# Gate and up weights of a two-expert MoE kernel in units of two k-tiles by 1024 columns, and the narrow expert's halves summed after transposes

## The chip, the cores and the metric

The kernel runs on one core of a Trainium2 chip. The metric is device time in microseconds (us), lower is better. The engines are named as in the profile: PE is TensorE (matmuls), PEld its weight loads, DVE VectorE, ACT ScalarE, POOL GpSimd, and SP the engine that issues the DMAs.

## The reference

A trunk of two layers on 256 tokens of width 1024, all in float32. Each layer has a token mixer (latent attention and stick-breaking attention) and a channel mixer. Layer 0's channel mixer is a dense SwiGLU. Layer 1's, in which the change lies, routes each token to two of eight experts of inner width 3584:

```python
def swiglu(x, w_gate, w_up, w_down):
    return (jax.nn.silu(x @ w_gate) * (x @ w_up)) @ w_down
...
    for e in range(N_EXPERTS):
        out = out + combine[:, e:e + 1] * swiglu(t, w_gate[e], w_up[e], w_down[e])
```

`w_gate[e]` and `w_up[e]` are 1024 by 3584, `w_down[e]` is 3584 by 1024, so one expert holds 44 MB and the eight hold 352 MB.

## The kernel before

**Precision.** A float32 product is made of single-pass products: a weight is split into a high part (ACT, `pair_hi_of`, L576) and a low part, raw minus high (DVE, `pair_lo_of`, L1262); the activations are split likewise. `product` (L1594 to L1596) issues high x high, high x low and low x high, three matmuls.

**Pairs.** Experts are handled in four pairs. The first of a pair is the wide one (`L`): up to 128 tokens, stationary operands `hg_hi` and `hg_lo`, 12 matmuls of 512 columns a unit. The second is the narrow one (`S`): up to 64 tokens, whose high and low halves stand side by side in one 128-wide stationary operand (`gs_pack`, later `f_pack`), so that a unit takes 8 matmuls; the two halves of its result stand in partitions 0 to 63 and 64 to 127 and must be added. Two overflow paths for fuller experts exist and are not run here.

**Units.** Weights come as units of 1 MB (128 partitions x 2048 floats), 42 to an expert and 84 to a pair. A gate or up unit is four k-tiles by 512 columns, so each partition gets four pieces of 2 KB; a down unit is two adjacent rows for each partition, one piece of 8 KB. SP issues one DMA a unit into a ring of seven raw buffers (`RAW`), each free again when its low part is made. The split parts go into four buffers (`PAIR_SPLIT`: three of `w_hi`/`w_lo` and `more_hi`/`more_lo`): the high part of unit j waits until PE has used unit j-4.

**Order.** `pair_order` lists the units for all engines. For each of seven chunks of 512 inner columns it has, wide expert first and then narrow: gate (2 units), up (2), and from chunk 1 on the down units of the chunk before (2). Both experts' last down units close the pair. So wide and narrow units alternate in runs of six. SP, ACT, DVE and PE each walk this list; the other work of ACT and DVE is hung behind the split of a certain unit (the `if u == ...` lines of their `pair`), and an engine does nothing else while it waits for such an item's input.

**Between the units.** For the wide expert: SiLU from PSUM (ACT L787), times up (DVE L1422), four transposes (PE L2000, `turn_l`), high part (ACT L791), low part (DVE L1426). For the narrow expert: both results are copied out of PSUM (ACT L796, L800), and `fold_s` (PE L2010) adds the halves and transposes in one step by eight float32 matmuls against a 0/1 matrix `fold`; then SiLU (ACT L804), times up (DVE L1432), high part (DVE L1437), low part (DVE L1439). Once in a pair come: the gather of the next wide tokens (`gather_l`, L1928, two halves), the gather of the narrow ones (`gather_s`, L1937), the scatter of the pair before (`scatter`, L1958 to L1961) with the weighting before it and four additions behind it (DVE L1412, L1414), and two selections (L1945, L1947) with the DVE's choice of the next pair's tokens (L1470, L1332).

**Start.** The first wide expert of all is the same whatever the routing says, so its units may be loaded early; before the first narrow unit SP must read the order of the experts (`order_i`, L480).

## Time and profile before

| | us |
|---|---|
| median of 3 runs | 1449.53 (1449.0 to 1451.09) |
| the profiled execution's own time | 1446.6 |
| its span (first to last instruction) | 1444.9 |
| PE busy / DVE busy / ACT busy | 1362.8 / 1261.7 / 940.7 |

The MoE of layer 1 runs from about 523 us to the end. "Busy" counts a matmul from its start to its modelled end, though the next one starts earlier; what a matmul costs in a stream is therefore the distance between two starts, not its duration. DVE and ACT instructions overlap a little too, by about 0.08 and 0.1 us.

### The profile page before, as it was taken

How to read it: one execution, taken by the hardware profiler on the slowest of the kernel's cores; microseconds unless marked ns; L12 is line 12 of the kernel's file. 1: busy time of each engine (PE TensorE's matmuls, PEld its weight loads, DVE VectorE, ACT ScalarE, POOL GpSimd, SP SyncE). 2: the span in 40 equal slices, each digit the busy share in tenths (PEclk: the TensorE clock that was granted, in tenths of full speed). 3: DMA queues.
4: the chain of work that ended last, by engine and by line, in shares of the span. 5: the costliest groups of instructions: out<-in, count | busy, mean ns of one | idle time of the engine just before them, and what ended most of it. 6: DMA issues, size and time to landing. Idle time of an engine off the chain costs nothing.

```text
span 1444.9 us, 18313 instructions
## 1 busy us (share of the span) xinstructions
PE 1362.8 (94%) x7090; PEld 1142.0 (79%) x7090; DVE 1261.7 (87%) x1141; ACT 940.7 (65%) x875; POOL 3.8 (0%) x35
## 2 busy tenths in 40 slices
PE   2899889999999889999999999999999999999995
PEld 2777789998887668887788887888888888888884
DVE  6878789887767779999998999998999998999997
ACT  1645443333437368878786888777878887877784
POOL 1000000000000000000000000000000000000000
PEclk9898999999899989999999999999999999999998
DMA  8973469987563139999999999999999999999992
GB/s 329 359 255 133 146 236 323 333 319 249 173 218 113 59 137 396 397 400 396 396 401 391 388 396 400 398 400 374 379 400 396 396 405 392 363 397 398 399 401 96
DMA packets 189596, 467.24 MB, mean 323 GB/s; under 512 B 8734, under 2 KB 10940, under 8 KB 175164
## 3 DMA queue, kind: packets, MB, share of 16 engines
q1 hardware_dynamic: 189500, 465.98, 86.3%
q8 instruction: 58, 0.95, 0.3%
q14 instruction: 38, 0.31, 0.1%
HBM read 464.90 MB, written 1.05 MB: 322 GB/s over the span
## 4 chain that ended last, share of the span: by engine, by line
PE 81%; DVE 8%; DMA 6%; ACT 3%; issue 1%; SPq 0%; DVEq 0%; ACTq 0%
PE bank L1594 17%; PE bank L1596 16%; PE bank L1595 16%; PE bank L1991 5%; PE bank L1992 5%; PE bank L2010 3%; PE bank L2034 3%; PE bank L2036 3%; DMA raw<-in_w_ex_down 3%; DVE w_lo L1262 3%; DMA raw<-in_w_ex_gate 2%; ACT w_hi L576 1%; DVE ring_sum L991 1%; PE bank L1928 1%; PE bank L1637 1%; PE bank L1615 1%
## 5 line engine op out<-in xcount | busy, mean ns | idle before, releaser
L1262 DVE TENSOR_TENSOR w_lo<-raw,w_hi 128x2048 fp32r<-128x2048 f32 x252 | 570.1, 2288 | 57.6 <-ACT w_hi L576 56.6
L576 ACT ACTIVATE w_hi<-raw 128x2048 fp32r<-128x2048 f32 x252 | 479.6, 1918 | 114.5 <-PE bank L1596 68.1
L1262 DVE TENSOR_TENSOR more_lo<-raw,more_hi 128x2048 fp32r<-128x2048 f32 x84 | 191.9, 2285 | 2.9 <-ACT more_hi L576 2.9
L552 ACT ACTIVATE w_hi<-raw 128x2048 fp32r<-128x2048 f32 (+1 forms) x54 | 102.3, 1897 | 130.5 <-PE bank L1596 121.4
L576 ACT ACTIVATE more_hi<-raw 128x2048 fp32r<-128x2048 f32 x84 | 161.3, 1920 | 33.6 <-PE bank L1596 20.3
L920 DVE TENSOR_TENSOR w_lo<-raw,w_hi 128x2048 fp32r<-128x2048 f32 (+1 forms) x54 | 121.7, 2258 | 19.6 <-ACT w_hi L552 19.4
L1594 PE MATMUL bank<-w_hi,hg_hi 128*128 128x512 f32 x336 | 136.5, 406 | 2.2 <-DVE w_lo L1262 1.6
L1991 PE MATMUL bank<-w_hi,gs_pack 128*128 128x512 f32 x336 | 135.2, 402 | 0.0
L1596 PE MATMUL bank<-w_hi,hg_lo 128*128 128x512 f32 x336 | 132.9, 396 | 0.0
L1595 PE MATMUL bank<-w_lo,hg_hi 128*128 128x512 f32 x336 | 132.9, 395 | 0.0
L1992 PE MATMUL bank<-w_lo,gs_pack 128*128 128x512 f32 x336 | 132.7, 395 | 0.0
L1594 PE MATMUL bank<-h_hi,w_hi 128*128 128x256 f32 x448 | 128.3, 286 | 1.6 <-DVE gate_m L969 1.6
L1595 PE MATMUL bank<-h_lo,w_hi 128*128 128x256 f32 x448 | 126.8, 283 | 0.0
L1596 PE MATMUL bank<-h_hi,w_lo 128*128 128x256 f32 x448 | 126.7, 283 | 0.0
L1594 PEld LDWEIGHTS bank<-h_hi,w_hi 128*128 128x128 f32 x448 | 86.0, 192 | 4.2 <-DVE gate_m L969 3.2
L1594 PE MATMUL bank<-w_hi,e_hi 128*128 128x512 f32 x224 | 88.9, 397 | 0.0
L1595 PE MATMUL bank<-w_lo,e_hi 128*128 128x512 f32 x224 | 88.6, 396 | 0.0
L1596 PE MATMUL bank<-w_hi,e_lo 128*128 128x512 f32 x224 | 88.6, 395 | 0.0
L1595 PEld LDWEIGHTS bank<-h_lo,w_hi 128*128 128x128 f32 x448 | 86.1, 192 | 0.7 <-issue 0.5
L1596 PEld LDWEIGHTS bank<-h_hi,w_lo 128*128 128x128 f32 x448 | 85.9, 192 | 0.0
L1594 PEld LDWEIGHTS bank<-w_hi,hg_hi 128*128 128x128 f32 x336 | 63.2, 188 | 21.6 <-issue 6.3
L991 DVE SCALAR_TENSOR_TENSOR ring_sum<-raw,cols,ring_sum 128x512 f32<-128x512 f32 x98 | 73.6, 751 | 3.3
(316 smaller groups left out, 2470.5 us busy)
## 6 DMA issues: line engine op xcount, KB each, us to landing
raw<-in_w_ex_gate SPq DMA_DIRECT2D x112, 1024.0 KB, 11.9
raw<-in_w_ex_up SPq DMA_DIRECT2D x112, 1024.0 KB, 12.3
raw<-in_w_ex_down SPq DMA_DIRECT2D x112, 1024.0 KB, 12.7
raw<-in_w_ada SPq DMA_DIRECT2D x48, 1024.0 KB, 7.0
raw<-in_w_in SPq DMA_DIRECT2D x12, 1024.0 KB, 6.5
raw<-in_w_ff_gate SPq DMA_DIRECT2D x10, 1024.0 KB, 7.0
raw<-in_w_ff_up SPq DMA_DIRECT2D x10, 1024.0 KB, 6.9
raw<-in_w_ff_down SPq DMA_DIRECT2D x10, 1024.0 KB, 6.3
```

Of the source, the lines that this page charges most:

```text
L552: act_e.activation(w_hi[:, s % SPLIT, 0:words], raw[:, n % RAW, 0:words], ACT.Copy).then_inc(hi_done, 1)
L576: act_e.activation(dst, raw[:, (N0 + n) % RAW, :], ACT.Copy).then_inc(hi_done, 1)
L920: dve.tensor_tensor(w_lo[:, s % SPLIT, 0:words], raw[:, n % RAW, 0:words], w_hi[:, s % SPLIT, 0:words].bitcast(F32), ALU.subtract).then_in ...
L991: ins = dve.scalar_tensor_tensor(out=dst, in0=w[:, k, :], scalar=ck, in1=dst, op0=ALU.mult, op1=ALU.add)
L1262: dve.tensor_tensor(lo, raw[:, (N0 + n) % RAW, :], hi.bitcast(F32), ALU.subtract).then_inc(lo_done, 1)
L1594: mm(o, lh, rh, start=first, stop=False, skip_group_check=True)
L1595: mm(o, lh, rl, start=False, stop=False, skip_group_check=True)
L1596: return mm(o, ll, rh, start=False, stop=last, skip_group_check=True)
L1991: mm(bank[b][:, :], gs_pack[:, kk, :], wh[:, k, :], start=kk == 0, stop=False, skip_group_check=True)
L1992: last = mm(bank[b][:, :], gs_pack[:, kk, :], wl[:, k, :], start=False, stop=kk == 7, skip_group_check=True)
L2010: last = mm(bank[2][:, o:o + HALF], pre[:, a * P:(a + 1) * P], fold[:, :], start=(i, a) == (0, 0), stop=True, skip_group_check=True)
L2034: mm(bank[6 + half][:, :], f_pack[:, kk, :], wh[:, k, cs], start=c == 0 and kk == 0, stop=False, skip_group_check=True)
```

## The change

Gate and up units become two k-tiles by 1024 columns: each partition gets two pieces of 4 KB. The inner width is cut into blocks of 1024, 1024, 1024 and 512 columns (`blocks`); the last keeps four k-tiles by 512. A block of 1024 has four gate, four up and four down units, so wide and narrow units now alternate in runs of eight (block 0), twelve (blocks 1 and 2) and eight (block 3), with two and two down units at the end. An accumulator is two PSUM banks wide; a pair of banks is gate accumulator, target of the transposes and narrow accumulator by turns. SiLU, the product, the evacuations and the splits of a block are one instruction 1024 wide. `turn_l` makes eight transposes a block and stands ahead of the narrow gate units instead of behind them.

`fold_s` still runs once for each 512 columns, now as eight transposes of 128 x 128; the halves then stand in adjacent columns, ACT copies the lower ones out (`keep_low_part`) and DVE adds (`sum_s`). The high part of the narrow activation moves from DVE to ACT (`high_s`). Folds 0 and 1 follow wide units of block 1, folds 2 to 5 the first and the fourth narrow down unit of blocks 1 and 2, fold 6 the first narrow down unit of block 3; copy and sum come four units behind a fold, SiLU and product six, the split eight. In block 1 and 2 the second fold waits for the first one's sum. Evacuations, gathers and selections are hung on other units; `add_rows` goes behind the second narrow up unit of block 0. The SBUF for this comes from a smaller scratch area for DMAs issued by POOL, of which there are none.

```diff
+    blocks = [(0, 4), (1024, 4), (2048, 4), (3072, 2)]
+    NB, LAST_B = len(blocks), len(blocks) - 1
     pair_order = []
-    for c in range(EC):
+    for b, (_, n) in enumerate(blocks):
         for who in "LS":
-            pair_order += [(who, kind, c, half) for kind in ("gate", "up") for half in range(2)]
-            if c > 0:
-                pair_order += [(who, "down", c - 1, half) for half in range(2)]
-    pair_order += [(who, "down", EC - 1, half) for who in "LS" for half in range(2)]
+            pair_order += [(who, kind, b, i) for kind in ("gate", "up") for i in range(n)]
+            if b > 0:
+                pair_order += [(who, "down", b - 1, i) for i in range(blocks[b - 1][1])]
+    pair_order += [(who, "down", LAST_B, i) for who in "LS" for i in range(blocks[LAST_B][1])]
     PU = len(pair_order)
     pair_at = {u: j for j, u in enumerate(pair_order)}
+    last_of = lambda who, kind, b: pair_at[who, kind, b, blocks[b][1] - 1]
+    fold_after = {0: pair_at["L", "gate", 1, 1], 1: pair_at["L", "up", 1, 0], LAST: pair_at["S", "down", LAST_B - 1, 0]}
+    for b in range(1, LAST_B):
+        fold_after[2 * b], fold_after[2 * b + 1] = pair_at["S", "down", b - 1, 0], pair_at["S", "down", b - 1, 3]
+    fold_at = {j: c for c, j in fold_after.items()}
+    sum_at = {j + 4: c for c, j in fold_after.items()}
+    silu_at = {j + (6 if c < LAST else 5): c for c, j in fold_after.items()}
+    split_f_at = {j + (8 if c < LAST else 6): c for c, j in fold_after.items()}
+    fold_banks = (6, 2, 0, 2)
+    gather_bank = lambda n, half: 3 if half == 0 else (2 if n == 0 else 1)
...
-        bank = [ctx.enter_context(nc.psum_tensor(f"bank{i}", [P, 512], F32)) for i in range(8)]
+        two_banks = [ctx.enter_context(nc.psum_tensor(f"banks{2 * i}", [P, 1024], F32)) for i in range(4)]
+        bank = [two_banks[i // 2][:, (i % 2) * 512:(i % 2 + 1) * 512] for i in range(8)]
...
+        def gate_banks(b):
+
+
+            return of_block(two_banks[b % 2], b)
+
+        def up_banks(b):
+
+            return of_block(two_banks[1 - b % 2], b)
+
+        def narrow_up_banks(b):
+
+            return gate_banks(b) if b < LAST_B else bank[3]
...
+                else:
+                    w = w_ex_gate if kind == "gate" else w_ex_up
+                    k = KD // units
+                    src = w[0, bass.ds(e, 1), i * k * P:(i + 1) * k * P, c0:c0 + UNIT // k].rearrange(
+                        "o (k p) n -> p (o k) n", p=P)
+                    dst = raw[:, slot, :].rearrange("p (k n) -> p k n", k=k)
...
+                def keep_low_part(c):
+
+                    act_e.wait_ge(folded, p * EC + (c + 1))
+                    if p > 0 or c > 1:
+                        act_e.wait_ge(flo_done, p * EC + c - 1)
+                    parts = two_banks[fold_banks[c // 2] // 2][:, :].rearrange("p (k t) -> p k t", t=P)
+                    act_e.activation(f_sum[:, c % 2, :, :], parts[:, :, HALF:P], ACT.Copy).then_inc(flow_kept, 1)
 
                 def silu_s(c):
-                    act_e.wait_ge(folded, p * EC + (c + 1))
-                    act_e.activation(f_act[:, :, :], bank[2][:, 0:4 * HALF].rearrange("p (k t) -> p k t", t=HALF),
-                                     ACT.Silu).then_inc(fsilu, 1)
+                    act_e.wait_ge(fsum_done, p * EC + (c + 1))
+                    act_e.activation(f_sum[:, c % 2, 0:4, :], f_sum[:, c % 2, 0:4, :], ACT.Silu).then_inc(fsilu, 1)
+
+                def high_s(c):
+                    act_e.wait_ge(fact_done, p * EC + (c + 1))
+                    act_e.activation(f_pack[:, 4 * (c % 2):4 * (c % 2) + 4, 0:HALF], f_sum[:, c % 2, 0:4, :],
+                                     ACT.Copy).then_inc(fhi_done, 1)
...
                         pair_hi_of(p, j)
+                    if j in sum_at:
+                        keep_low_part(sum_at[j])
+                    if j in silu_at:
+                        silu_s(silu_at[j])
+                    if j in split_f_at:
+                        high_s(split_f_at[j])
...
+                def sum_s(c):
+
+                    dve.wait_ge(flow_kept, p * EC + (c + 1))
+                    parts = two_banks[fold_banks[c // 2] // 2][:, :].rearrange("p (k t) -> p k t", t=P)
+                    dve.tensor_tensor(f_sum[:, c % 2, :, :], parts[:, :, 0:HALF], f_sum[:, c % 2, :, :],
+                                      ALU.add).then_inc(fsum_done, 1)
 
                 def gated_s(c):
 
                     dve.wait_ge(fsilu, p * EC + (c + 1))
-                    dve.tensor_tensor(f_act[:, :, :], f_act[:, :, :],
-                                      bank[2][:, 4 * HALF:8 * HALF].rearrange("p (k t) -> p k t", t=HALF),
+                    dve.tensor_tensor(f_sum[:, c % 2, 0:4, :], f_sum[:, c % 2, 0:4, :], f_sum[:, c % 2, 4:8, :],
                                       ALU.mult).then_inc(fact_done, 1)
-                    dve.wait_ge(fact_done, p * EC + (c + 1))
-                    h, l = f_pack[:, :, 0:HALF], f_pack[:, :, HALF:P]
-                    dve.tensor_copy(h, f_act[:, :, :]).then_inc(fhi_done, 1)
+
+                def low_s(c):
+                    k = slice(4 * (c % 2), 4 * (c % 2) + 4)
                     dve.wait_ge(fhi_done, p * EC + (c + 1))
-                    dve.tensor_tensor(l, f_act[:, :, :], h.bitcast(F32), ALU.subtract).then_inc(flo_done, 1)
+                    dve.tensor_tensor(f_pack[:, k, HALF:P], f_sum[:, c % 2, 0:4, :], f_pack[:, k, 0:HALF].bitcast(F32),
+                                      ALU.subtract).then_inc(flo_done, 1)
 
...
                 def fold_s(c):
 
-                    pe.wait_ge(gate_kept, p * EC + (c + 1))
-                    pe.wait_ge(up_kept, p * EC + (c + 1))
+                    b, o = c // 2, 512 * (c % 2)
+                    pe.wait_ge(gate_kept, p * NB + (b + 1))
+                    pe.wait_ge(up_kept, p * NB + (b + 1))
+                    if c == 0 and p > 0:
+                        pe.wait_ge(acc_done, p * 4)
+                    if c % 2 == 1:
+                        pe.wait_ge(fsum_done, p * EC + c)
+                    if b == LAST_B:
+                        pe.wait_ge(elo_done, p * NB + (b + 1))
                     for i, pre in enumerate((g_pre, u_pre)):
                         for a in range(4):
-                            o = (4 * i + a) * HALF
-                            last = mm(bank[2][:, o:o + HALF], pre[:, a * P:(a + 1) * P], fold[:, :], start=(i, a) == (0, 0),
-                                      stop=True, skip_group_check=True)
+                            last = pe.transpose(bank[fold_banks[b] + i][:, a * P:(a + 1) * P],
+                                                pre[:, o + a * P:o + (a + 1) * P], ident[:, :])
                     last.then_inc(folded, 1)
 
-                def down_l(c):
-                    for pair_of in range(2):
-                        pe.wait_ge(elo_done, p * EC + (c + 1))
-                        wh, wl = unit(("L", "down", c, pair_of))
...
+                def done(u, last):
+                    last.then_inc(split_used, 1)
+                    if pair_at[u] in fold_at:
+                        fold_s(fold_at[pair_at[u]])
...
+                for b, (_, units) in enumerate(blocks):
+
+                    if p > 0 or b > 0:
+                        pe.wait_ge(gate_kept, p * NB + b)
+                    for i in range(units):
+                        into_l("gate", b, i, gate_banks(b))
+
+                    if b == 1:
+                        pe.wait_ge(up_kept, p * NB + 1)
+                    elif p > 0 or b > 0:
+                        pe.wait_ge(fsum_done, p * EC + 2 * b)
+                    for i in range(units):
+                        into_l("up", b, i, up_banks(b))
+                        if (b, i) == (0, 1):
+                            pe.wait_ge(esilu, p * NB + (b + 1))
+                            gather_s(p)
+                        if (b, i) == (SEL_L, 2):
...
                     else:
-                        if c == 1 and p > 0:
+                        if b == 1 and p > 0:
                             pe.wait_ge(acc_done, p * 4)
-                        down_l(c - 1)
-                        pe.wait_ge(flo_done, p * EC + c)
-                    into_s("gate", c, 2)
-                    turn_l(c)
-                    if c == SEL_L:
-                        selection(sel, now, tl_ready)
-                    if c == SEL_S:
-                        selection(sel_s, now_s, ts_ready)
-                    if c == LAST and p + 1 < PAIRS:
...
-                fold_s(LAST)
-                if p + 1 < PAIRS:
-                    gather_l(p + 1, 1)
-                down_l(LAST)
-                down_s(LAST)
+                        if b == LAST_B and p + 1 < PAIRS:
+                            gather_l(p + 1, 0)
+                            gather_l(p + 1, 1)
+                        for i in range(blocks[b - 1][1]):
+                            down_l(b - 1, i)
+                    if b == SEL_L:
+                        pe.wait_ge(tl_done, p * 2 + 2)
+                    if b == SEL_S:
+                        pe.wait_ge(ts_done, p * 2 + 2)
+                    turn_l(b)
+                    for i in range(units):
+                        into_s("gate", b, i, up_banks(b))
+                    if b < LAST_B:
+                        pe.wait_ge(elo_done, p * NB + (b + 1))
+                    elif p + 1 < PAIRS:
+                        pe.wait_ge(hgl_done, (p + 1) * 2 + 1)
+                    for i in range(units):
+                        into_s("up", b, i, narrow_up_banks(b))
+                    if b > 0:
+                        for i in range(blocks[b - 1][1]):
+                            down_s(b - 1, i)
+                for i in range(blocks[LAST_B][1]):
+                    down_l(LAST_B, i)
```

PE, around the second fold of a block. Before, in chunk 2 of the first pair (`hg_hi` marks wide units, the fold is L2010):

```order
L2010 MATMUL bank<-fold,g_pre 128x64 x4
L2010 MATMUL bank<-fold,u_pre 128x64 x4
L1594 MATMUL bank<-w_hi,hg_hi 128x512
L1595 MATMUL bank<-w_lo,hg_hi 128x512
L1596 MATMUL bank<-w_hi,hg_lo 128x512
```

After, at the end of block 1's narrow run (`f_pack` marks narrow down units):

```order
L2121 MATMUL banks<-more_hi,f_pack 128x512
L2123 MATMUL banks<-more_lo,f_pack 128x512
L2060 MATMUL banks<-ident,g_pre 128x128 x4
L2060 MATMUL banks<-ident,u_pre 128x128 x4
L1669 MATMUL banks<-w_hi,hg_hi 128x512
```

A fold is still eight rows of PE's order; it stood among wide units and now stands between narrow down units or behind the last of them.

DVE, in the narrow run of chunk 1 and the wide one of chunk 2 before (the splits are L1262, `more_lo` is every fourth of them):

```order
L1439 TENSOR_TENSOR f_pack<-f_act,f_pack 128x4x64
L1262 TENSOR_TENSOR w_lo<-raw,w_hi 128x2048 x2
L1422 TENSOR_TENSOR e_act<-e_act,bank 128x512
L1262 TENSOR_TENSOR more_lo<-raw,more_hi 128x2048
L1262 TENSOR_TENSOR w_lo<-raw,w_hi 128x2048
L1470 COPY now<-place 128x4
L1332 TENSOR_SCALAR sel<-slot_no,now 128x128 x2
L1262 TENSOR_TENSOR w_lo<-raw,w_hi 128x2048 x2
L1426 TENSOR_TENSOR e_lo<-bank,e_hi 128x512
```

After, from the fourth narrow unit of block 1 to the sum behind its first narrow fold (`f_sum<-banks`):

```order
L1326 TENSOR_TENSOR more_lo<-raw,more_hi 128x2048
L1492 TENSOR_TENSOR e_lo<-banks,e_hi 128x1024
L1326 TENSOR_TENSOR w_lo<-raw,w_hi 128x2048
L1544 COPY now<-place 128x4
L1396 TENSOR_SCALAR sel<-slot_no,now 128x128 x2
L1326 TENSOR_TENSOR w_lo<-raw,w_hi 128x2048 x2
L1326 TENSOR_TENSOR more_lo<-raw,more_hi 128x2048
L1326 TENSOR_TENSOR w_lo<-raw,w_hi 128x2048 x3
L1326 TENSOR_TENSOR more_lo<-raw,more_hi 128x2048
L1326 TENSOR_TENSOR w_lo<-raw,w_hi 128x2048
L1499 TENSOR_TENSOR f_sum<-banks,f_sum 128x512
```

From the fourth narrow unit to the sum there are ten splits, one `e_lo`, one choice of tokens and the sum.

## Rows read from the trace of the kernel before

**Rows 1.** Pairs 1, 2: length, busy PE PEld DVE ACT POOL, clock, DMA share, GB/s.

```profile
757.93:982.93 225.00, 224.63 (x1075) 184.09 (x1074) 210.73 (x137) 177.91 (x131) 0.00 (x0) 1.00 1.04 395
982.93:1208.10 225.17, 224.65 (x1075) 184.09 (x1074) 211.09 (x137) 178.15 (x131) 0.00 (x0) 1.00 1.03 391
```

**Rows 2.** Chain of waits that ended last: start us, us, what.

```profile
522.96 6.50 PE bank L1928 x32
...
757.93 3.52 PE bank L1937 x32
...
907.52 1.73 PE bank L2010 x16
...
924.25 0.44 PE bank L2000 x4
...
938.03 1.73 PE bank L2010 x16
...
955.19 1.79 PE bank L1928 x16
...
966.16 1.84 PE bank L1928 x16
...
1002.01 2.39 DVE acc L1414 x4
...
1425.93 0.70 ACT ye_hi L756
```

**Rows 3.** PE in order of time: start us, us, instruction, from 700 us.

```profile
700.29 0.40 PE L1991 MATMUL bank<-w_hi,gs_pack 128*128 128x512 f32 x1
...
701.92 0.39 PE L1992 MATMUL bank<-w_lo,gs_pack 128*128 128x512 f32 x1
...
704.77 0.47 PE L2034 MATMUL bank<-more_hi,f_pack 128*128 128x512 f32 x1 [0.59 <-DVE more_lo L1262]
```

**Rows 4.** PE in order of time, the selection of pair 2.

```profile
1026.72 0.38 PE L1945 MATMUL bank<-ident,sel 128*128 128x128 f32 x2
...
1027.31 0.48 PE L1991 MATMUL bank<-w_hi,gs_pack 128*128 128x512 f32 x1
```

**Rows 5.** DVE in order of time.

```profile
702.34 2.28 DVE L1262 TENSOR_TENSOR more_lo<-raw,more_hi 128x2048 fp32r<-128x2048 f32 x1
...
1029.18 0.68 DVE L1426 TENSOR_TENSOR e_lo<-bank,e_hi 128x512 fp32r<-128x512 f32 x1
1029.78 2.28 DVE L1262 TENSOR_TENSOR more_lo<-raw,more_hi 128x2048 fp32r<-128x2048 f32 x1
...
1038.59 2.29 DVE L1262 TENSOR_TENSOR more_lo<-raw,more_hi 128x2048 fp32r<-128x2048 f32 x1
...
1055.07 0.16 DVE L1470 COPY now<-place 128x4 f32<-128x4 f32 x1
...
1055.66 4.49 DVE L1262 TENSOR_TENSOR w_lo<-raw,w_hi 128x2048 fp32r<-128x2048 f32 x2
```

**Rows 6.** ACT in order of time.

```profile
1045.30 1.92 ACT L576 ACTIVATE w_hi<-raw 128x2048 fp32r<-128x2048 f32 x1 [0.73 <-PE bank L1596]
1048.10 1.92 ACT L576 ACTIVATE more_hi<-raw 128x2048 fp32r<-128x2048 f32 x1 [0.88 <-PE bank L1596]
```

**Rows 7.** Groups of one pair period by form, DVE and ACT: busy us, mean ns.

```profile
L1439 DVE TENSOR_TENSOR f_pack<-f_act,f_pack 128x256 fp32r<-128x256 f32 x7 | 3.0, 426 | 0.2
...
L791 ACT ACTIVATE e_hi<-bank 128x512 fp32r<-128x512 f32 x7 | 4.1, 591 | 0.0
...
L804 ACT ACTIVATE f_act<-bank 128x256 f32<-128x256 f32 x7 | 2.7, 383 | 5.5 <-PE bank L2010 5.5
```

**Rows 8.** DMA, 600 to 700 us: GB/s in slices of 2.5 us.

```profile
GB/s 419 390 385 389 384 414 420 390 389 385 387 401 421 408 390 384 390 383 420 423 383 389 384 389 407 423 406 380 388 386 392 421 402 393 385 388 385 425 423 381
```

**Rows 9.** SP: its first DMAs of a narrow unit, and its wait before them.

```profile
527.42 0.96 SPq L459 DMA_DIRECT2D raw<-in_w_ex_gate  x2
...
SPq L480 <- DVE order_i L1365: 35.8, 1, 35.8
```

More of the change, by code:

```diff
@@ L1457, in pair @@
[L1457 to L1467 removed]
+                    if u[0:2] == ("L", "down") and i == 2:
+                        gated_l(b + 1)
@@ new lines, in turn_l, with down_l @@
+                def turn_l(b):
+                    pe.wait_ge(ea_done, p * NB + (b + 1))
+                    for a in range(2 * blocks[b][1]):
+                        last = pe.transpose(gate_banks(b)[:, a * P:(a + 1) * P], e_act[:, a * P:(a + 1) * P], ident[:, :])
+                    last.then_inc(e_tp, 1)
+                def down_l(b, i):
+                    pe.wait_ge(elo_done, p * NB + (b + 1))
+                    wh, wl = unit(("L", "down", b, i), 2)
+                    for half in range(2):
+                        for k in range(2):
+                            kk = 2 * i + k
+                            cs = slice(half * 512, (half + 1) * 512)
+                            last = product(bank[4 + half][:, :], e_hi[:, kk, :], e_lo[:, kk, :], wh[:, k, cs], wl[:, k, cs],
+                                           b == 0 and kk == 0, b == LAST_B and kk == 3)
+                    done(("L", "down", b, i), last)
```

334 lines of the change are left out of this document (161 added, 173 removed).

## The prediction

> **What bounds the kernel now.** I read the stretches of the pairs first. A middle pair lasts 225.0 or 225.2 us, and in it PE is busy for 224.6, DVE for 210.7 and ACT for 177.9, while the DMA engines are at full share with 391 to 395 GB/s [rows 1]. The chain of waits runs almost wholly along PE [rows 2]. So PE sets the pace, DMA and DVE stand close behind, and ACT has room.
>
> Next, what PE does with a pair, by the distance between starts. In a stream a matmul of 512 columns starts each 0.233 us (seven steps in 1.63 us, [rows 3]), so a wide unit costs 12 x 0.233 = 2.80 and a narrow one 8 x 0.233 = 1.87. A pair has 42 of each: 195.7 us. Seven folds of 1.73 are 12.1, seven times four transposes of 0.44 are 3.1, the two halves of gather_l 1.79 + 1.84 = 3.6, gather_s 3.5 [rows 2], the scatter's 16 matmuls 3.7, two selections of 0.59 each 1.2 [rows 4]. The sum is 222.9, so PE waits for about 2.2 us a pair. A chunk shows where: from fold to fold it takes 938.03 - 907.52 = 30.5 us [rows 2], its work 6 x 2.80 + 6 x 1.87 + 1.73 + 0.44 = 30.2, which leaves 0.3, six times a pair.
>
> These waits can be derived, and I use the derivation for the new order too. The split of a unit needs a buffer that PE has left four units earlier. Let t = 0 be the moment at which a narrow run begins. ACT learns of a used buffer 0.3 later (a matmul's duration of 0.40 against 0.233, and a hand-over of 0.15, which is what lies between the end of a low part, 702.34 + 2.28, and the matmul at 704.77) [rows 3, 5]. The fourth narrow unit's high part therefore runs from 0.3 to 2.2 (1.92 each, [rows 6]) and its low part starts at 2.25. From there DVE needs 2.20 for each split (8.81 for four) and 0.60 for e_lo [rows 5]. In the old run of six, DVE still has four splits and one e_lo to do before the next wide unit can start: 2.25 + 8.8 + 0.6, and 0.23 for its last end and the hand-over, is 11.9; PE's own work is 0.44 + 6 x 1.87 = 11.65. Wait 0.25: the trace has 0.3.
>
> **The change, part by part.**
>
> The folds. Eight transposes take the place of eight float32 matmuls. Four transposes cost 0.44 [rows 2], so eight are 0.88 against 1.73: 0.85 x 7 = 5.95 us a pair, 24 in all. The bounds are 0.88 (nearest row, taken) and 1.73 (as before, nothing won). turn_l keeps its 28 transposes a pair. PE's own work falls to 216.9.
>
> The DMAs. The bandwidth goes up and down with the units: about 387 GB/s for two thirds of the time, about 420 for one third [rows 8], which is how 2 KB gate/up pieces and 8 KB down pieces share a pair. A unit thus takes 1.049 MB / 387 = 2.71 or 2.50 us, and a pair 56 x 2.71 + 28 x 2.50 = 221.8. A 4 KB piece is not in these rows; its bounds are the two rates. At the better one the floor falls to 8 x 2.71 + 76 x 2.50 = 211.7, at the worse it stays. Both are below the pair length found below, and DMA has seven raw buffers to even things out, so I put this part at 0. What it should do is end most of ACT's waits for DMA.
>
> The Trainium skill ("DMA: Bandwidth & Descriptors", section "Where 436 GB/s comes from") says that a load from HBM is limited to about 358 GB/s a core; by that a pair's 88.1 MB would need 246 us and nothing on PE could help. The trace disagrees, with 391 to 395 GB/s over whole pairs [rows 1], and the measurement decides.
>
> DVE and ACT. DVE loses the high part of f (0.3 x 7) and gains a sum of the size of e_lo (0.60 x 7); for e_act and e_lo I need 1024 columns: 256 take 0.43 and 512 take 0.68 [rows 5, 7], so 1024 take about 1.20 by the slope (two separate ones, 1.36, is the other bound), 1.12 from start to start. DVE stays near 212 us a pair. ACT gains a copy of 0.59 and one of 0.38 for each fold and loses some overhead, about 5 us a pair on 178 [rows 1, 7]. Averages thus say nothing: 217 on PE, 212 on DVE, 212 on DMA, 183 on ACT.
>
> The longer runs. Here the gain goes. In a run of twelve wide units DVE is ahead but can bank only four buffers; in a run of twelve narrow ones PE needs a unit each 1.87 and DVE makes one each 2.20. Blocks 1 and 2: turn_l now stands first (0.88), then eight narrow units, the ninth, a fold, three more, the second fold. Ahead of the second fold PE's own work is 0.88 + 12 x 1.87 + 0.88 = 24.2. That fold waits for the first one's sum, and DVE's order has, from 2.25 on, ten splits (22.0), e_lo (1.12), the choice of tokens (0.59, [rows 5]) and the sum (0.60), then 0.23: 26.8. PE loses 2.6 in each of the two blocks, most of it spread over single units, the last 0.9 at the fold. The next wide unit is ready by then.
>
> Block 0: the scatter (3.7) hides the product gated_l. After it PE has 0.88 + 8 x 1.87 = 15.8. The fifth narrow unit's high part waits for the first to be used (0.88 + 1.87 + 0.3 = 3.05), its low part ends at 7.2; then come a split, add_rows (2.39, [rows 2]), and three splits up to the next wide unit: 7.2 + 2.2 + 2.4 + 6.6 + 0.23 = 18.6. Loss 2.8. Block 3 with the closing down units: PE 0.44 + 8 x 1.87 + 0.88 + 5.6 + 3.7 = 25.6; DVE 2.25 + ten splits 22.0 + e_lo 0.6 + sum 0.6 + product and low part 0.7 + 0.23 = 26.4. Loss 0.8. Together 2.8 + 2.6 + 2.6 + 0.8 = 8.8 against 2.2 before. I keep 0.4 for what my derivation does not explain now (2.2 less six times 0.3): 216.9 + 8.8 + 0.4 = 226.1, 1.0 more than before.
>
> The other pairs. Pair 0 goes from 529.5 (the end of gather_l) to 757.9 - 5.6 = 752.3, 222.9 us. After: no scatter, so 213.2, but turn_l now has nothing to hide behind: gated_l follows the low part of the third narrow unit, whose high part may start 2.8 before the wide run ends; it is done 3.4 after that end, so PE loses 3.5; then 0.3 instead of 2.8 (no add_rows), 5.2, 0.8, 0.4: 223.4, 0.5 more. In this pair SP stops for 35.8 us for the order of the experts and goes on at 527.4 [rows 9]; four units are in by then, after the change seven or eight, so DMA can't hold it up. The last pair goes from 1208.1 - 5.6 to 1425.9, 223.4 us. After: no gather_l, 213.3; waits 2.8, twice 2.0 (no choice of tokens), 0.4 at the end, where the f work no longer stands behind the last split, and 0.4: 220.9, 2.5 less.
>
> **The sum.** 0.5 + 1.0 + 1.0 - 2.5 = 0: 24 us won on the folds, 24 lost in waits. The profiled execution took 1446.6 (span 1444.9 and 1.7 around it), and the median is 1449.5, 2.9 higher; I forecast 1450 for the median.
>
> **Rivals.**
>
> A: PE keeps its pace. If the narrow runs cost no more waiting than now (2.2 a pair), all 24 us are won: 1426. For it: PE is 99.8% busy and DVE's queue shows idle 14 us a pair [rows 1]. Against it: these 14 us lie in the wide runs, where DVE waits for buffers. Half of it gives 1438.
>
> B, slower: DMA paces the narrow runs. Twelve units at 2.50 to 2.71 are 30 to 32.5 us against my 27.7 (26.8 and the fold). If the seven raw buffers are nearly empty when a narrow run begins, each of the blocks 1 and 2 loses about 4 more: 8 x 4 = 32, 1482. It decides at about two landed units. For it: DMA is at full share now. Against: PE's waits and gathers leave it 4 to 14 us a pair after the change.
>
> C, slower: a fold's transposes of g_pre and u_pre cost as much as its matmuls did; then the waits partly cover it (the fold's end matters twice a block): about +15, 1465.
>
> D: PE's clock. The granted clock is 1.00 in both pairs [rows 1] though each has 32 transposes and small waits. If it fell to 1.2 GHz in the narrow runs for a third of their length, each run of twelve would lose 7 us: over 1490. The Trainium skill ("TensorE: Matmul & The Clock Gate", section "Part 4: PE-mode transpose") says that transposes don't count as PE activity the way matmuls do; the change adds 56 of them a pair and waits next to them. By that rule D would come; the transposes of the present kernel bear nothing of it out.
>
> **Chances.** Forecast 0.58 (own range 1444 to 1457), A 0.24, B 0.10, C 0.05, D 0.03. About 0.2% (2.9 us) is what a measurement can tell from no change. The forecast's share splits into faster 0.10, same 0.27, slower 0.21, since each wait may be wrong by 0.5 us and there are 13 of them. Faster is then 0.34, same 0.27, slower 0.39. The range 1434 to 1464 takes in the upper half of A and the lower edge of C and leaves out about 0.2.
>
> **What would show it.** Right: folds of about 0.88; PE waiting for low parts in the second half of narrow runs and for the sum before each second narrow fold, 7 to 10 us a pair; ACT's waits for DMA nearly gone and a DMA share below 1; narrow runs of blocks 1 and 2 near 27.7 us. Wrong: PE's waits at 2 to 4 us a pair (A), ACT waiting for DMA in narrow runs (B), folds of 1.7 (C), a granted clock below 1 there (D).

## The result, and the profile after

The changed kernel takes 1457.89 us (median of 4 runs, 1457.07 to 1458.39); the kernel before, on the same chip, 1449.26 (4 runs). The ratio is 1.0065, 95% interval 1.005 to 1.008: slower by 8.6 us, where I had forecast no change. The profiled executions are 1457.07 and 1446.6.

First the stretches of pairs 1 and 2, from one gather of the narrow rows to the next, as in [rows 1] (columns: length, busy PE, PEld, DVE, ACT, POOL with their instructions, granted clock, DMA share, GB/s):

```profile
771.91:999.30 227.39, 221.65 (x1017) 176.26 (x1016) 212.08 (x131) 182.63 (x132) 0.00 (x0) 1.00 0.98 382
999.30:1226.70 227.40, 221.66 (x1017) 176.25 (x1016) 211.97 (x131) 182.64 (x132) 0.00 (x0) 1.00 0.99 388
```

A middle pair has grown by 2.3 us, though its seven folds have 56 matmuls fewer. PE is no longer busy all the time, and the DMA share has gone from 1.04 to 0.98. The chain of waits that ended last, over the whole kernel and by engine, was 81% PE, 8% DVE and 6% DMA before. Now:

```profile
PE 65%; DVE 29%; ACT 4%; issue 1%; DMA 1%; SPq 0%; DVEq 0%; ACTq 0%
```

In its order of time it shows a fold of eight transposes with 0.87, where [rows 2] has 1.73. In the narrow run of block 1 in pair 2 it follows DVE for 26 us, up to the second fold, which waits for the first one's sum:

```profile
581.83 0.87 PE banks L2060 x8
...
1067.09 1.93 ACT more_hi L621
1069.04 2.29 DVE more_lo L1326
1071.34 1.14 DVE e_lo L1492
1072.47 2.20 DVE w_lo L1326
1074.78 0.48 DVE sel L1396 x2
1075.27 4.40 DVE w_lo L1326 x2
1079.67 2.20 DVE more_lo L1326
1081.87 6.60 DVE w_lo L1326 x3
1088.48 2.20 DVE more_lo L1326
1090.68 2.20 DVE w_lo L1326
1092.88 0.61 DVE f_sum L1499
1093.63 1.07 PE banks L2060 x8
```

This is the prediction's derivation almost item by item: the fourth unit's high part, ten splits of 2.20, e_lo with 1.14 (1.12 taken), the choice of tokens, the sum with 0.61 (0.60 taken). ACT's waits for DMA among all waits of 560 to 1410 us are four lines with 3.1 us in all; before it was 43.4 us.

```profile
ACT more_hi L621 <- DMA raw<-in_w_ex_up: 1.3, 2, 0.6
...
ACT w_hi L621 <- DMA raw<-in_w_ex_up: 0.7, 1, 0.7
...
ACT more_hi L621 <- DMA raw<-in_w_ex_gate: 0.6, 1, 0.6
...
ACT w_hi L621 <- DMA raw<-in_w_ex_gate: 0.5, 1, 0.5
```

**Where the difference lies.** The beginning of the pair stage is a poor anchor: PE's first wide unit starts between 528.6 and 534.4 us in the fourteen profiled executions, though the code ahead of it is the same. So all executions below are measured by the *pair stage*, from the start of the first wide unit to the first matmul of the last scatter. It is 900.4 us before (529.22 to 1429.59) and 909.8 after (528.57 to 1438.38): 9.4 more. The rest of the 10.5 us between the two profiled executions lies outside it: 0.7 less ahead of the stage and 1.7 more behind its end. Pair by pair, first wide unit to first wide unit (for the last pair to the end of its units):

| | before | predicted | after |
|---|---|---|---|
| pair 0 | 222.9 | 223.4 | 226.5 |
| pairs 1 and 2, each | 225.1 | 226.1 | 227.4 |
| last pair | 223.4 | 220.9 | 223.2 |
| then PE's wait before the scatter | 3.7 | 3.7 | 5.2 |

The misses are 3.1 + 1.3 + 1.3 + 2.3 + 1.5 = 9.5 us. Most of them come from three things that the prediction lacks, each with its rows here.

First, a wait in block 3, in every pair. PE in order of time at the end of block 2 and in block 3 of pair 2, and DVE beside it:

```profile
1155.60 0.63 PE L2060 MATMUL banks<-ident,g_pre 128*128 128x128 f32 x4 [0.70 <-DVE f_sum L1499]
...
1163.05 0.50 PE L1669 MATMUL banks<-w_hi,hg_hi 128*128 128x512 f32 x1 [0.79 <-DVE f_sum L1499]
```

```profile
1160.11 2.28 DVE L1326 TENSOR_TENSOR more_lo<-raw,more_hi 128x2048 fp32r<-128x2048 f32 x1
1162.32 0.68 DVE L1499 TENSOR_TENSOR f_sum<-banks,f_sum 128x512 f32<-128x512 f32 x1
```

Block 3 has two gate units instead of four. Its first wide up unit therefore reaches the banks of fold 5 when DVE has only now come to that fold's sum, which stands four units behind it. Start to start, the matmul comes 0.95 us late.

Second, TensorE's clock. In pair 0 the turn of the wide product waits 3.4 us, as predicted (3.5). But the matmuls after it are 0.43 us apart instead of 0.233, which goes with the lower of the clock's two levels (1.2 instead of 2.4 GHz). The chain shows the distance, and the stretches of 3 us show the granted clock (the column behind POOL):

```profile
559.79 0.43 PE banks L2091
560.21 0.43 PE banks L2092
```

```profile
552.00:555.00 3.00, 2.77 (x12) 1.88 (x10) 0.99 (x1) 2.53 (x3) 0.00 (x0) 1.00 1.00 400
555.00:558.00 3.00, 0.00 (x0) 0.00 (x0) 3.00 (x4) 1.78 (x1) 0.00 (x0) 1.00 0.34 87
558.00:561.00 3.00, 2.82 (x12) 2.56 (x13) 2.36 (x3) 1.02 (x1) 0.00 (x0) 0.59 0.82 311
561.00:564.00 3.00, 3.00 (x13) 2.40 (x12) 1.11 (x1) 1.21 (x1) 0.00 (x0) 0.84 0.89 281
564.00:567.00 3.00, 3.00 (x15) 2.41 (x14) 2.25 (x2) 3.00 (x3) 0.00 (x0) 1.00 0.17 68
```

The eight transposes behind the wait take 1.60 here, where `a_last` and `a_five` below, with the clock at 1.00, have 1.06 and 1.07. From the first of these transposes to the end of 25 matmuls it is 8.3 us, in those two 6.7: the fall costs 1.6 us. Behind block 0's wait of 2.0 us in the last pair the same thing costs 1.5 us (eight matmuls at 0.43), with the clock at 0.65 and 0.79 from 1254 to 1260; pairs 1 and 2 have two small waits at this place instead, 0.5 us together.

Third, the tail. DVE's last split ends 2.2 us before PE's last unit does, and behind it stand the two sums over acc and x, ahead of the low parts that the scatter needs:

```profile
1428.65 2.29 DVE L1326 TENSOR_TENSOR more_lo<-raw,more_hi 128x2048 fp32r<-128x2048 f32 x1
1430.86 2.29 DVE L1563 TENSOR_TENSOR acc<-acc,gate_f 128x2048 f32<-128x2048 f32 x1
1433.18 2.29 DVE L1565 TENSOR_TENSOR x<-x,acc 128x2048 f32<-128x2048 f32 x1
1435.51 1.41 DVE L1448 SCALAR_TENSOR_TENSOR ye_lo<-banks,w_slot,ye_hi 128x512 fp32r<-128x512 f32 x2
```

Before, DVE came to these two sums 4 us before PE's last unit ended, and they cost nothing.

### The profile page after: what moved, and what is told of

It is laid out like the page before. It is cut to its first block, busy times and chain, and to the rows that moved or that the text cites. A ratio compares the mean times of both kernels' runs of the same rounds, so it can differ in the third digit from the quotient of the medians.

```text
span 1455.3 us, 17840 instructions
## 1 busy us (share of the span) xinstructions
PE 1351.9 (93%) x6866; PEld 1113.4 (77%) x6866; DVE 1265.6 (87%) x1117; ACT 958.2 (66%) x883; POOL 3.2 (0%) x32
## 4 chain that ended last, share of the span: by engine, by line
PE 65%; DVE 29%; ACT 4%; issue 1%; DMA 1%; SPq 0%; DVEq 0%; ACTq 0%
PE banks L1669 17%; PE banks L1671 17%; PE banks L1670 17%; DVE w_lo L1326 16%; DVE more_lo L1326 7%; ACT more_hi L621 2%; DVE ring_sum L1055 1%; PE banks L2003 1%; PE banks L1712 1%; PE banks L1690 1%; PE banks L2012 1%; PE banks L1869 1%; DVE e_lo L1492 1%; DMA raw<-in_w_ada 1%; PE banks L2060 1%
## 5 line engine op out<-in xcount | busy, mean ns | idle before, releaser
L2091 PE MATMUL banks<-w_hi,gs_pack 128*128 128x512 f32 x336 | 137.0, 408 | 8.1 <-DVE w_lo L1326 7.5
L1669 PE MATMUL banks<-w_hi,hg_hi 128*128 128x512 f32 x336 | 135.5, 403 | 3.8 <-DVE f_sum L1499 3.2
L2092 PE MATMUL banks<-w_lo,gs_pack 128*128 128x512 f32 x336 | 133.9, 398 | 0.0
L1671 PE MATMUL banks<-w_hi,hg_lo 128*128 128x512 f32 x336 | 132.8, 395 | 0.0
L1670 PE MATMUL banks<-w_lo,hg_hi 128*128 128x512 f32 x336 | 132.8, 395 | 0.0
L1669 PE MATMUL banks<-h_hi,w_hi 128*128 128x256 f32 x448 | 128.2, 286 | 1.6 <-DVE gate_m L1033 1.6
L1670 PE MATMUL banks<-h_lo,w_hi 128*128 128x256 f32 x448 | 126.7, 283 | 0.0
L1671 PE MATMUL banks<-h_hi,w_lo 128*128 128x256 f32 x448 | 126.7, 283 | 0.0
L1669 PEld LDWEIGHTS banks<-h_hi,w_hi 128*128 128x128 f32 x448 | 86.0, 192 | 4.3 <-DVE gate_m L1033 3.2
L1670 PEld LDWEIGHTS banks<-h_lo,w_hi 128*128 128x128 f32 x448 | 86.0, 192 | 0.7 <-issue 0.5
```

What stands on the lines that cost most here:

```text
L1669: mm(o, lh, rh, start=first, stop=False, skip_group_check=True)
L1670: mm(o, lh, rl, start=False, stop=False, skip_group_check=True)
L1671: return mm(o, ll, rh, start=False, stop=last, skip_group_check=True)
L2091: mm(at[:, cs], gs_pack[:, kk, :], wh[:, k, cs], start=kk == 0, stop=False, skip_group_check=True)
L2092: last = mm(at[:, cs], gs_pack[:, kk, :], wl[:, k, cs], start=False, stop=kk == 7, skip_group_check=True)
```

## The experiments

Each ratio is to the kernel before on the same chip; the stage is the pair stage of the profiled execution (before 900.4, after 909.8).

**1 to 3: the parts of the change in the old order.** `b_half_fold` takes half of each fold away from the kernel before (0.87 us, about what the transposes save; the product takes the gate part twice); `b_4kb` gives it the new pieces; `b_both` has both.

```
-   for i, pre in enumerate((g_pre, u_pre)):          b_half_fold
+   for i, pre in enumerate((g_pre,)):
+   if c < EC - 1:                                    b_4kb
+       r0 = (2 * (c % 2) + half) * 256
+       src = w[0, bass.ds(e, 1), r0:r0 + 256, c // 2 * 1024:(c // 2 + 1) * 1024]   # two k-tiles
```

> The kernel before, with one edit: fold_s does only its four matmuls on g_pre, and the product takes the gate part twice, so u_pre is not folded. PE's work falls by 0.87 a fold, as it does with eight transposes, and nothing is added on ACT or DVE; the order of the units and the 2 KB pieces stay. Theory (PE sets the pace and the DMA floor of 221.8 us a pair lies 3 us below it): pairs of 222 us instead of 225, 12 us less in all (9 to 15), ACT waiting for DMA more than now. Rival (the DMA floor doesn't bind): pairs of 219, 24 us less.

> The kernel before, with one edit: the gate and up units of chunks 0 to 5 are loaded as two k-tiles by 1024 columns, 4 KB pieces, the same bytes of HBM in all as the changed kernel reads, but used as if they were four k-tiles by 512, so the values are wrong and the work on them is the same. Theory (PE sets the pace before, DMA is hidden but for part of pair 0): 0 to 4 us less, ACT's waits for DMA nearly gone. Rival (DMA paces the kernel before): pairs of 212 to 216 us, 36 us or more less.

> Both edits together on the kernel before: half a fold, and 4 KB pieces used as if they were 2 KB ones (wrong values, same work). Theory (two limits close together, each hides the other): pairs of 219 us, 24 us less in all (20 to 28), clearly more than the two edits alone add up to. Rival (something else, DVE or ACT, already stands at 222): no more than half the fold alone gives, 9 to 15 us less.

Measured: 1446.8 (ratio 0.9978, 0.996 to 0.9996), 1445.42 (0.998, 0.9963 to 0.9997) and 1425.64 (0.9827, 0.9791 to 0.9863); stages 899.0, 898.2, 879.0. So each part alone is worth 1 to 3 us (medians, ratios and stages differ by that much), and both together 22.6. In `b_half_fold` my theory failed by its size, 12 us expected: as soon as PE needs less, DMA paces the kernel. Its middle pair, and ACT's three longest waits for DMA (us in total, times, longest):

```profile
756.78:979.98 223.20, 219.44 (x1019) 177.38 (x1018) 211.22 (x137) 178.33 (x131) 0.00 (x0) 1.00 1.04 396
```

```profile
ACT w_hi L576 <- DMA raw<-in_w_ex_up: 34.0, 44, 0.8
ACT w_hi L576 <- DMA raw<-in_w_ex_gate: 22.8, 43, 0.8
ACT w_hi L576 <- DMA raw<-in_w_ex_down: 20.8, 34, 1.2
```

This is close to the floor of 221.8 us a pair that the prediction worked out for 2 KB pieces: the gathers of the narrow rows of the four pairs lie 222.1, 223.2 and 224.6 us apart. In `b_4kb` ACT has no wait for DMA left, and the page's slices of 36 us, in which 4 KB and 8 KB pieces stand mixed, read 412 to 414 GB/s at the start of the pair stage (the sixteenth to nineteenth of forty). [rows 8] alternates between about 387 and 420:

```profile
GB/s 331 359 257 131 146 246 312 334 314 255 171 216 117 59 140 412 414 413 413 401 409 326 403 414 412 400 386 344 395 413 411 405 384 371 366 411 411 406 404 40
```
With both:

```profile
751.53:971.06 219.53, 218.67 (x1019) 177.69 (x1018) 210.13 (x137) 178.28 (x131) 0.00 (x0) 1.00 1.02 404
971.06:1190.68 219.62, 218.64 (x1018) 177.68 (x1018) 210.19 (x137) 178.09 (x131) 0.00 (x0) 1.00 1.01 401
```

The middle pairs are 5.5 us shorter than before, against the 5.95 that the folds were said to save. DMA is close again: ACT's waits for it are 39.9 us in all. The change has both savings too, and its stage is 30.8 us longer than this one's. What differs is the order of the work, runs of six there and of up to twelve here, with other items between the splits. No run has the long runs without the other items, so how the 30.8 us share out between the two is not shown.

**4: what a fold costs now.** The transposes of each fold made twice:

```
-   for i, pre in enumerate((g_pre, u_pre)):
+   for i, pre in 2 * list(enumerate((g_pre, u_pre))):
```

> The changed kernel, with every fold's eight transposes made twice: 0.87 us more PE work a fold, 6.1 a pair, 24 in all. Theory (in the narrow runs of blocks 1 and 2 DVE paces, so PE work ahead of a wait costs nothing): folds 2 and 4 are covered by the wait of the fold that follows, fold 5 by the wait of the wide up unit behind it, fold 6 half; the rest shows: 3 us a pair, 12 in all (9 to 15) over the changed kernel, 1470. Rival (PE paces everywhere): 24 us over it, 1482.

Measured: 1469.0 (1.0136, 1.0097 to 1.0176), 11 us above the changed kernel; stage 920.4. A fold of sixteen reads 1.75 in the chain. Rival C is out: the folds are at 0.87, and what they save is real, since giving it back costs 11 us, near the 12 expected, even with waits beside it.

**5, 6: the reserve of split buffers.** `PAIR_SPLIT` 3 and 5 for 4, in the changed kernel.

> The changed kernel with three pairs of split buffers (hi and lo) instead of four in the pair stage, nothing else. Theory (in a narrow run VectorE makes a split every 2.25 us and TensorE uses a unit up every 1.75, so every run of ten or more narrow units ends in waits, shortened by what the buffers hold in reserve at its start): one buffer less is one split less in reserve, 2.2 us more of waiting in each of the three full narrow runs of a pair and 1 to 2 in the short fourth: 8 us a pair, 33 on the kernel, 1491. Rival (reserve is not what it is about; TensorE waits for what stands between the splits, folds and row additions): under 8 us more, at most 1466.

> The changed kernel with five pairs of split buffers instead of four, the space taken from x and from one of the seven raw buffers (six are left); it leaves the residual x out of the last sum. Theory: one more split in reserve takes up to 2.2 us of waiting from each of the three full narrow runs, which now wait 2.6 to 2.9 us; 6 to 7 us a pair, so that the middle pairs take 220.5 to 221.5 us instead of 227.4, 25 us on the kernel, 1433. Against it stands the raw buffer that is missing: a transfer has one unit (1.8 us) less of lead. Rival (the waits follow VectorE's order of work, not its reserve): the middle pairs keep 225 us or more.

Measured: 1549.96 with three (1.0703, 1.0685 to 1.0721), 1446.04 with five (0.9992, 0.9977 to 1.0006); stages 1000.6 and 897.0. The direction is the theory's in both, but both sizes are wrong. With three the kernel loses 92 us, not 33, and the rival's 8 are out. (The paces in its expectation, 2.25 and 1.75, are not the trace's: it has 2.20 and 1.87.) DVE's waits for a high part grow from 47 us to 129 (first line), and ACT's share of the chain from 4% to 8%:

```profile
DVE w_lo L1326 <- ACT w_hi L621: 129.4, 118, 6.7
```

```profile
PE 65%; DVE 24%; ACT 8%; issue 2%; DMA 1%; SPq 0%; DVEq 0%; ACTq 0%
```

An estimate from the prediction's numbers says why: with three buffers a high part is ready 1.87 + 0.3 + 1.92 = 4.1 us after the low part three units before it, and DVE wants it after 2 x 2.20 = 4.4. So nearly every copy or SiLU of ACT in between delays it, and my derivation has DVE alone in the line. No run takes ACT's items out of it. With five the stretches of pairs 0 to 2 are:

```profile
548.53:768.23 219.70, 215.74 (x1002) 173.99 (x1001) 205.68 (x125) 181.59 (x132) 0.00 (x0) 1.00 1.00 395
768.23:992.24 224.01, 220.06 (x1018) 176.77 (x1017) 211.38 (x131) 180.13 (x132) 0.00 (x0) 1.00 0.99 389
992.24:1218.05 225.81, 220.23 (x1018) 176.76 (x1018) 212.46 (x131) 184.17 (x133) 0.00 (x0) 1.00 1.00 393
```

The first is 6.8 us shorter than in the changed kernel, but half of that is luck: 1.9 are a shorter wait at the turn (1.47 idle instead of 3.41) and 1.6 the fall of the clock, which doesn't come. The long narrow runs give 1.3 each and not 2.2: block 1 of pair 2 has one wait of 0.24 ahead of its second fold where there were 1.3, and the fold's own 0.9 stays. Pairs 1 and 2 are 3.4 and 1.6 us shorter; the second, 225.8, is what the rival said. There ACT's waits for DMA are back, with 43.5 us in all, and PE waits in wide units for what comes late by them, up to 1.4 us at a time. With six raw buffers and a high part wanted one unit earlier, the run can't say which of the two brings these waits, nor what five would give with seven raw buffers; there is no room for both.

**7, 8: single items.** `a_sum` makes the sum of fold 5 earlier; `a_add` moves the row additions from the narrow run to the wide one.

```
-   sum_at = {j + 4: c for c, j in fold_after.items()}                       a_sum
+   sum_at = {j + (2 if c == LAST - 1 else 4): c for c, j in fold_after.items()}
-   if u == ("S", "up", 0, 1) and p > 0:  add_rows(p - 1)                     a_add
+   if u == ("L", "gate", 1, 0) and p > 0:  add_rows(p - 1)
```

> The changed kernel with ScalarE's copy and VectorE's sum of fold 5 put two units behind the fold instead of four. Theory: in the last, short block the wide up unit that takes over the fold's banks waits 0.95 us for that sum in each pair, since VectorE comes to it only after a split that it makes too late; with the sum ahead, that wait goes in all four pairs: 3.8 us less, 1454. Rival (VectorE is behind there anyway, so that the wait turns up at the next unit): within 1 us of 1458.

> The changed kernel with VectorE's addition of a pair's rows to the sum (2.6 us of VectorE) moved from the first narrow run of the next pair to the wide run behind it. Theory: block 0's wait (2.9 us in the middle pairs, and 2.0 us in the last, behind which TensorE's granted clock fell and cost 1.6 more) goes but for 0.3 of it, for VectorE has time to spare in a wide run: 2.5 us in each of pairs 1 and 2, 3.5 in the last, 8.5 less, 1449. Rival (the wait is the narrow run's own shortfall and only shows behind the addition): pair 1 and 2 keep 226.5 us or more, 3 us less in all at most.

Measured: `a_sum` 1455.53 (1.0066, 1.0044 to 1.0087), stage 905.6, 4.2 less than after. In its trace the wait of 0.95 is gone from each pair and nothing comes in its place, so the first missed item is shown by the stage, with its size. The time of the whole kernel doesn't show it: the ratio is that of the changed kernel (1.0065). `a_add` 1456.44 (1.0067, 1.005 to 1.0084), stage 906.8, 3.0 less, and again no gain in the ratio. Its theory failed, and its rival was nearer. Block 0's wait of 2.0 is gone, but the next wide run has a new one:

```profile
1034.12 0.50 PE L1669 MATMUL banks<-w_hi,hg_hi 128*128 128x512 f32 x1 [1.47 <-DVE w_lo L1326]
```

At the end of a narrow run DVE has nothing in hand, and it gets only 0.6 us ahead for each wide unit (2.80 less 2.20). An item right behind the run costs nearly what it cost in it, here 1.6 instead of 2.0. In the last pair the clock stayed at 1.00 behind this shorter wait, and there 1.5 us were won.

**9 to 12: putting them together.** `a_p0` moves the first pair's product. `a_most` has `a_sum`, `a_p0`, the choice of tokens late in the next wide run, and the tail's two sums in wide runs of the last pair. `a_best` adds the row additions, four units into the wide run, and folds 0 and 1 two units later. `a_last` corrects the first pair:

```
-   if u == ("S", "up", SEL_L, 0) and p + 1 < PAIRS:           a_most
+   if u == ("L", "up", SEL_L + 1, 3) and p + 1 < PAIRS:
-   if u == ("S", "up", SEL_S, 0) and p + 1 < PAIRS:
+   if u == ("L", "down", SEL_S, 1) and p + 1 < PAIRS:
-   if u == ("S", "up", 0, 1) and p > 0:                       a_best (add_rows)
+   if u == ("L", "gate", 1, 3) and p > 0:
-   fold_after = {0: pair_at["L", "gate", 1, 1], 1: pair_at["L", "up", 1, 0],
+   fold_after = {0: pair_at["L", "gate", 1, 3], 1: pair_at["L", "up", 1, 2],
-   if u == ("S", "gate", 0, 2):                               a_last (evacuate_s, split_s, gated_l)
+   if u == ("S", "gate", 0, 1 if p == 0 else 2):
```

> The changed kernel in which, in the first pair alone, VectorE makes block 0's wide product behind the split of the second narrow gate unit; it stood behind the third and behind the split of the gathered narrow rows. Theory (the first pair is 3 us longer than the sum had it because TensorE waits 3.6 us at the turn of the wide product and its granted clock then falls to 0.59 for a few us, which costs 2 more): the product is ready about 3.4 us sooner, the wait is under 0.5 us, the clock stays at 1.00, and the first pair (from its first gather of narrow rows to the next) takes 221.5 to 222.5 us instead of 226.5: 4.5 us less, 1453.5. Rival 1 (the fall of the clock has nothing to do with the wait): 3 us less, and matmuls 0.43 us apart are there still. Rival 2 (VectorE's work is only shifted, and the wait turns up at the end of the narrow run): under 1.5 us less.

> The changed kernel with four moves on VectorE: the sum of fold 5 two units behind the fold; the first pair's product as in a_p0; the choice of tokens for the next pair taken out of the narrow runs and put late into the next wide run (blocks 2 and 3), where VectorE waits 0.5 us before each split; and in the last pair the two sums over acc and x, 2.3 us each, out of the tail into the wide runs of blocks 2 and 3. Theory, by its terms: 1.0 us in each of four pairs, 4.5 in the first pair, 0.6 to 0.7 in each of two narrow runs of three pairs, 1.5 in the tail: 4 + 4.5 + 3.9 + 1.5 = 13.9 less, 1444; middle pairs 225.1 instead of 227.4. Rival (work moved on VectorE comes back as a wait a run later, as it did where the row additions were moved): half of it, 1451, middle pairs 226.3 or more.

> As a_most, and VectorE's addition of the rows moved into the wide run of block 1, not at its start, where it cost 1.6 us of the 2.0 that it saved, but behind the split of its fourth unit, with folds 0 and 1 two units later so that they need not wait for it. Theory (what decides is whether VectorE has got ahead again before the work comes: four wide units give back 0.5 us each): of block 0's 2.9 us of waiting 2.0 go in each of pairs 1 to 3, at most 0.7 comes back in the wide run, and in the last pair the fall of the clock behind that wait goes too (1.6 us): 5.5 less than a_most, 1438.5. Rival (nothing is got ahead, the wait only moves): within 2 us of a_most.

> As a_best, with another order in the first pair's block 0: ScalarE's copy and VectorE's low part of the gathered narrow rows, and then the wide product, all one unit earlier (behind the second narrow gate unit). In a_p0 and a_best the product alone was moved, and TensorE's wait at the turn grew from 3.6 to 4.4 us, for TensorE waits there for the low part of the narrow rows too, which then stood behind the product and another split. Theory: with neither of them behind the third split, whose buffer TensorE frees only after the gather, the wait falls from 4.4 to about 1.4 us, which is the product alone; with a wait that short TensorE's granted clock stays at 1.00 there (0.9 us of matmuls 0.43 us apart go as well): the first pair 221.5 instead of 225.0, the kernel 1440.5. Rival (the third split, made later, is then what TensorE waits for in the narrow run): 1 us less at most, 1443.

| | us | ratio, interval | stage | middle pair |
|---|---|---|---|---|
| a_p0 | 1458.73 | 1.0069, 1.005 to 1.0089 | 910.5 | 228.2, 227.4 |
| a_most | 1453.01 | 1.003, 1.0014 to 1.0046 | 904.2 | 226.0 |
| a_best | 1443.99 | 0.9964, 0.9951 to 0.9978 | 895.2 | 222.7 |
| a_last | 1440.05 | 0.9949, 0.9932 to 0.9966 | 891.3 | 222.7 |

`a_p0` failed outright: nothing was won, and the theory had said 4.5 us. PE waits there for the low part of the gathered narrow rows as well, and I had pushed that part behind the product and a split, one that can't be made before the gather is over. The releaser named at that wait was e_act in the changed kernel and is gs_pack in `a_p0` and in `a_best`, whose line this is:

```profile
561.28 1.97 PE L2110 MATMUL banks<-ident,e_act 128*128 128x128 f32 x8 [4.19 <-DVE gs_pack L1466]
```

With both items ahead of that split, `a_last` has:

```profile
562.12 1.06 PE L2107 MATMUL banks<-ident,e_act 128*128 128x128 f32 x8 [1.47 <-DVE e_act L1487]
```

Its eight transposes take 1.06 instead of 1.97, no matmul behind them is at 0.43, and the first pair takes 221.0 us from gather to gather, where `a_best` has 225.0 (221.5 was expected). `a_best` shows that work on DVE can be moved for good if it comes where DVE is ahead: the middle pairs fall by 3.3 against `a_most`, and no wait longer than 0.9 is left in them. In `a_most` the tail's wait is back at 3.7, so the third missed item is shown; its middle pairs sank by 1.4 instead of 2.3. So `a_most` as a whole, 1453.0, came nearer to its rival (1451) than to its theory (1444). `a_best` gained 9.0 on it instead of 5.5 and stayed at 1444.0, where 1438.5 had been expected; only `a_last` met its number, 1440.5. The wait of 0.5 that opened the series in blocks 1 and 2 is gone, as the choice of tokens in a better place should make it, but behind block 0's wait the clock fell in both of these pairs, where it hadn't in the changed kernel's:

```profile
1028.72 0.68 PE L2101 MATMUL banks<-w_hi,gs_pack 128*128 128x512 f32 x1 [1.85 <-DVE w_lo L1326]
1029.20 0.63 PE L2102 MATMUL banks<-w_lo,gs_pack 128*128 128x512 f32 x1
1029.62 0.63 PE L2101 MATMUL banks<-w_hi,gs_pack 128*128 128x512 f32 x1
```

That is also why `a_best`, which has no such wait, gains more in a middle pair than the 2.0 us expected of it.

`a_last` is 7.9 us under the kernel before, on the same chip, and 17.8 under the changed one. `b_both` is lower still, at 1425.64, but it leaves half of each fold out and multiplies by other weights than the reference's; what it shows is what the two savings are worth in the old order.

## Why the prediction was right, and where not

The forecast was 1450, no change, with slower the likeliest sign (0.39); measured is 1457.9, inside the range but 0.9 above the forecast's own narrower one (1444 to 1457). The mechanism was right: about 24 us won on the folds, and as much and more lost in waits, most of them in DVE's narrow runs. The zero was not: the sum left out some 9 us of waits, and the range took them in. Step by step:

- *PE sets the pace, DMA close behind.* Right, closer than I treated it: without the larger pieces the folds alone gain 1 to 3 us (`b_half_fold`). The floor of 221.8 holds. The Trainium skill's limit of about 358 GB/s a core for loads from HBM ("DMA: Bandwidth & Descriptors", "Where 436 GB/s comes from") is not borne out here, with one core running: over whole pairs it is 382 to 404 GB/s in the changed kernel, the kernel before and `b_both`.
- *Folds 0.88, 24 us.* Right: 0.87; the edits of `b_both` gained 22.6 us, and taking the saving back in `a_fold_twice` cost 11 where 12 was expected.
- *DMA worth 0.* It fits the changed order, with 3 us of waits left at pairs of 227.4, but no run has that order with 2 KB pieces.
- *Waits of blocks 0, 1, 2: 2.8, 2.6, 2.6.* Right. In pair 2 the matmuls' starts come late by 2.0 + 0.2 + 0.3 and some tenths in block 0, and by 0.5 + 0.2 + 0.2 + 0.3 and 0.9 at the fold in each of blocks 1 and 2, with small ones about 2.8. These two narrow runs take 27.6 us each, 27.7 predicted.
- *Block 3: 0.8; and "The next wide unit is ready by then", behind the second folds.* The failed step. The end of block 3 has 0.3 + 0.2, and its first gate unit is ready, but not its first up unit: I looked for splits only and not for the sum of fold 5, which is due after two gate units in this block and is placed after four. It costs 0.95 in each of four pairs, 3.8 us; in `a_sum` it is gone.
- *Pair 0: the turn waits 3.5.* Right with 3.6, start to start; missed is the fall of the clock behind it, 1.6 us, and 1.5 in the last pair. Rival D had the clock fall in narrow runs for want of matmuls. That is not what happened: it stayed at 1.00 over both middle pairs with 88 transposes each. It fell only after PE had stood still. The Trainium skill ("TensorE: Matmul & The Clock Gate", "Part 4: PE-mode transpose") says that transposes don't count as PE activity the way matmuls do; in these pairs they brought no fall of their own.
- *Last pair, end.* The narrow runs there were right (1.7 each; 2.0 predicted). Missed are the two sums in the tail, 1.5 us: I had the queue behind the last split in mind for f, not for acc and x.

Together 3.8 + 1.6 + 1.5 + 1.5 = 8.4 of the 9.4 us of the stage; the last 1.0 is spread over steps too small to name.

Rival A failed with PE's waits at 8 to 10 us a pair instead of 2 to 4. Rival B did not come, with 3 us of waits for DMA; `b_half_fold` and `a_five` show how near it was. Rivals C and D are answered above: folds of 0.87, and a clock of 1.00 over the middle pairs.

## What to carry to other kernels

When two engines are within a few per cent of each other, a change that saves work on the one and lengthens the stretches in which the other is the slower can lose all that it saves, as here: work out for each stretch what the slower engine has in hand when it begins. Then look at every item that the new order makes due earlier, not at the main stream alone, above all in a block that is shorter than the others. And an item moved out of a stretch in which its engine is behind must go to where that engine has got ahead, which is not directly behind that stretch.

## What the runs showed of the hardware

TensorE's granted clock went to its lower level after the waits of 3.4 to 6.2 us at the first pair's turn, in all eight executions that had one. It did so in the last scatter of all fourteen, the kernel before too, behind waits of 3.7 to 7.6 us. After block 0's wait of 2.0 us it fell in some pairs and not in others: in one pair of three in the changed kernel, `a_fold_twice`, `a_p0` and `a_sum`, in two of three in `a_most`. It did not after the waits of 1.5 to 1.6 in `a_five`, `a_add` and `a_last`, nor after the three waits of 2.5 us inside block 0's narrow runs in `a_three`, so the length of a wait alone doesn't decide it. So a wait of some microseconds can have a price beside its length, here 1.5 to 1.6 us at a first pair's turn or in block 0.

Loads in 4 KB and 8 KB pieces mixed ran at 412 to 414 GB/s in `b_4kb`, with one core running; [rows 8], with 2 KB and 8 KB pieces, goes up and down between 387 and 420. A rate for 4 KB pieces alone was not measured.
